# ScalarE keeps the turned tokens of two tiles whole from PSUM, in place of GpSimd's sums of heads and rests

## The chip, the cores and the metric

One core of a Trainium2 chip runs the whole program. The time is device microseconds (us) of one execution; the median of the runs counts.

## What is computed

A decoder trunk of two layers on 512 tokens of width 1024, all in float32. Each layer has a mixer (attention of some kind with an output projection) and a gated MLP with a causal convolution of width 3. Each is followed by a residual and a LayerNorm:

```python
for i in range(DEPTH):
    m = even_mixer(x, ...) if i % 2 == 0 else odd_mixer(x, ...)
    x = layer_norm(DEEPNORM_ALPHA * x + m, ln_mix_g[i], ln_mix_b[i])
    f = conv_ffn(x, w_up[i], conv_w[i], conv_b[i], w_down[i])
    x = layer_norm(DEEPNORM_ALPHA * x + f, ln_ffn_g[i], ln_ffn_b[i])
```

`conv_ffn` multiplies by `w_up` (1024 x 5632), convolves along the tokens, forms silu(gate) * value and multiplies by `w_down`.

## The kernel before

**Heads and rests.** TensorE multiplies in a format with fewer bits than float32. So each operand is kept as a head (`_hi`, the rounded value) and a rest (`_lo`, the value less the head), and each product is three matmuls: head by head, head by rest, rest by head. For the weights, ScalarE makes the heads (`heads`, L490) and GpSimd the rests (`rest`, L336, in two halves of 1024 columns). The weights come from memory in steps, numbered through the program; AT_UP is the first step of the up projection in a layer, AT_UP+1 the second.

**The LayerNorms.** There are four, i = 0 to 3; i = 0 and 2 follow the mixers, and the MLP of the layer comes behind them. The 512 tokens are four tiles t = 0 to 3 of 128. On VectorE `norm(i)` goes, for each tile, through `norm_sum` (L948, residual plus product out of two banks, then the mean L955), `norm_mul` (L968, which reads `x` and `gain`), `norm_root` (L976, L979, L982, each one element wide) and `norm_out` (L991, which reads `ln_mul` and `shift` and gives `xn`). ScalarE makes the statistics in between (`norm_stats`, L514 to L520).

**Turning.** TensorE turns each normalised tile (`turn_x(i, t)`, L1376, eight transposes) into banks 2t and 2t+1. It waits for `xn` of the tile. ScalarE makes the heads `xt_hi` of the turned tokens (`xt_heads`, L507), VectorE the rests `xt_lo` (`xt_rests`, L934). The order of work on every engine is written out by hand: each engine runs its own list, in order, and waits on semaphores. VectorE's order in `norm` is: ... `norm_sum(2)`, `xt_rests(0)`, `xt_rests(1)`, `norm_mul(2)`, `norm_root(2)`, `norm_out(2)`, `norm_sum(3)`, `norm_mul(3)`, `norm_root(3)`, `norm_out(3)`, `xt_rests(2)`, `xt_rests(3)`.

**The up projection.** TensorE begins it while the last tiles are still being normalised: `first_columns` (L1434) multiplies step AT_UP with the first 256 tokens, unit 0, then turns tile 2, then unit 1; then `up_half(0, 0)` multiplies the first half of step AT_UP+1 with the same tokens into bank 2, tile 3 is turned, and `up_half(0, 1)` multiplies the second half into bank 3. Then the same follows for the other 256 tokens. A unit of 24 matmuls on 256 tokens is one such multiplication. All further steps (`up_body`) use a scheme with seven products instead of eight (two by two blocks, the tokens as left and right half, the 1024 inputs as low and high half), L1765. It needs sums and differences of weights and of tokens. The mixed tokens are T1 to T4 in `t_raw`, made on VectorE by `tokens_mixed` (L1239 to L1247) from the turned tokens of tiles 2 and 3 in banks 4 to 7, and from those of tiles 0 and 1. The latter are no longer in their banks by then. They stand in `x_raw`, 128 x 2 x 8 x 128 float32. GpSimd makes `x_raw` (`token_sum`, L432) as the sum of `xt_hi` and `xt_lo`, two operations of 128 x 1024 in each layer. The scheme's weights are the blocks W11, W12, W22 and four sums of blocks; their rests are made by GpSimd (`w_rest`, L445) and VectorE (L1258), their heads by ScalarE (L765; W11's first one at L921).

GpSimd's list around the change: the rests of AT_UP and AT_UP+1 (L336), a wait for `xn` of all four tiles, `token_sum(0)`, `token_sum(1)`, W11's rest (L445), then the rests of T3 and T4 of tile 2 and of tile 3 (L438), each after its head.

ScalarE's list around the change: `norm_stats(0)`, `norm_stats(1)`, `xt_heads(0)`, `xt_heads(1)`, `norm_stats(2)`, `heads(after + 1)` (this is step AT_UP+1), `norm_stats(3)`, `xt_heads(2)`, a load of the table for Silu (L916), W11's head (L921), `xt_heads(3)`, the copies out of banks 4 and 6 into `t_raw` (L839).

Of the kernel before, what the change touches and what calls it, by code (L numbers as in the profile page):

```python
# [22 lines left out]
F32 = mybir.dt.float32  # L23
F32R = mybir.dt.float32r
ACT = mybir.ActivationFunctionType
ALU = mybir.AluOpType

P = 128
# [4 lines left out]
NT = S // P  # L33
# [51 lines left out]
def build(nc, x_in, xt_in, w_stream, ident_in, rope_in, mask_in, tri_in, conv_in, ln_in, out):  # L85
    ctx = ExitStack()
    with ctx:
# [6 lines left out]
        bank = [ctx.enter_context(nc.psum_tensor(f"bank{b}", [P, 512], F32)) for b in range(8)]  # L94
# [7 lines left out]
        xt_hi = sb("xt_hi", [P, KD, S], F32R)  # L102
        xt_lo = sb("xt_lo", [P, KD, S], F32R)
# [7 lines left out]
        x = sb("x", [P, NT, D])  # L111
# [45 lines left out]
        with ExitStack() as st:  # L157
            sb("below_x_raw", [P, KF - 4, S], stack=st)
            x_raw = sb("x_raw", [P, 2, KD, P], stack=st)
# [169 lines left out]
        def _(pool):  # L329
# [29 lines left out]
            for l in range(DEPTH):  # L359
# [67 lines left out]

                w, u = W[l], U[l]

                def token_sum(j):  # L430
                    pool.wait_ge(T[2 * l + 1]["lo"], 2 * j + 2)
                    pool.tensor_tensor(x_raw[:, j, :, :], xt_hi[:, :, j * P:(j + 1) * P].bitcast(F32),  # L432
                                       xt_lo[:, :, j * P:(j + 1) * P].bitcast(F32), ALU.add).then_inc(w["x"], 1)

                def t_rest(row, j, seen):
                    part = slice(j * P, (j + 1) * P)
                    pool.wait_ge(*w.at("th", seen))
# [14 lines left out]
                    pool.tensor_tensor(h_all[:, f, :], sig[f % 2][:, :], cv[f % 2][:, :],  # L452
                                       ALU.mult).then_inc(u["h"], 1)

                pool.wait_ge(N[2 * l]["xn"], NT)
                token_sum(0)
                token_sum(1)
                w_rest(0, W11, w_raw[(b + AT_UP + FIRST) % 2][:, 0:Q])
                for j in range(2):
                    t_rest(T3, j, 4 * j + 1)  # L460
# [24 lines left out]
        def _(act):  # L485
# [18 lines left out]
            def xt_heads(i, t):  # L504
                act.wait_ge(T[i]["mm"], t + 1)
                for g in range(2):
                    act.activation(xt_hi[:, 4 * g:4 * g + 4, t * P:(t + 1) * P],  # L507
                                   bank[2 * t + g][:, :].rearrange("p (k q) -> p k q", k=4),
                                   ACT.Copy).then_inc(T[i]["hi"], 1)

            def norm_stats(i, t):
                n = N[i]
                act.wait_ge(n["mean"], t + 1)
                act.activation(ln_junk[:, :], x[:, t, :], ACT.Square, bias=stat[:, t, 2:3],  # L514
                               accum_out=stat[:, t, 3:4]).then_inc(n["sq"], 1)
                act.wait_ge(n["sq"], t + 1)
                act.activation(stat[:, t, 4:5], stat[:, t, 3:4], ACT.Ln, bias=eps[:, 0:1],
                               scale=4.0 / D).then_inc(n["lv"], 1)
                act.wait_ge(n["lv"], t + 1)
                act.activation(stat[:, t, 5:6], stat[:, t, 4:5], ACT.Exp, scale=-0.5).then_inc(n["y0"], 1)  # L520
# [155 lines left out]
            for l in range(DEPTH):  # L676
# [53 lines left out]
                w, u = W[l], U[l]  # L730
                for i, after in ((2 * l, b + AT_O + 4), (2 * l + 1, b + PER_LAYER)):
# [160 lines left out]
                    if i == 2 * DEPTH - 1:  # L892
                        def scaled(t):
                            act.wait_ge(N[i]["nt"], 2 * t + 2)
                            act.wait_ge(N[i]["mulg"], t + 1)
                            act.activation(x[:, t, :], product(i, t), ACT.Copy,
                                           scale=stat[:, t, 8:9]).then_inc(N_LAST["scaled"], 1)

                        norm_stats(i, 0)
                        norm_stats(i, 1)  # L900
                        scaled(0)
                        scaled(1)
                        norm_stats(i, 2)
                        norm_stats(i, 3)
                    else:
                        norm_stats(i, 0)
                        norm_stats(i, 1)
                        xt_heads(i + 1, 0)
                        xt_heads(i + 1, 1)
                        norm_stats(i, 2)  # L910
                        act.wait_ge(w_used, after - 1)
                        heads(after + 1, used=False)
                        norm_stats(i, 3)
                        xt_heads(i + 1, 2)
                        if i % 2 == 0:
                            act.preload_act_table(ACT.Silu)  # L916
                            first = after + FIRST
                            s, part = operand(l, W11)
                            act.wait_ge(raw_full[first % 2], filled(first, 0))
                            act.wait_ge(w_used, after)  # L920
                            act.activation(w_hi[s][:, part], w_raw[first % 2][:, 0:Q], ACT.Copy).then_inc(w["hi"], 1)  # L921
                        xt_heads(i + 1, 3)
                        if i % 2:
                            act.wait_ge(N[i]["xn"], NT)
                            load_gain(i + 1)
# [3 lines left out]
        def _(dve):  # L929
            def xt_rests(i, t):  # L930
                for g in range(2):
                    dve.wait_ge(T[i]["hi"], 2 * t + g + 1)
                    part = xt_hi[:, 4 * g:4 * g + 4, t * P:(t + 1) * P]
                    dve.tensor_tensor(xt_lo[:, 4 * g:4 * g + 4, t * P:(t + 1) * P],  # L934
                                      bank[2 * t + g][:, :].rearrange("p (k q) -> p k q", k=4),
                                      part.bitcast(F32), ALU.subtract).then_inc(T[i]["lo"], 1)

            def norm_sum(i, t, halves=(0, 1)):

                n = N[i]  # L940
                for g in halves:
                    if (i, t, g) == (0, 0, 0):
                        dve.wait_ge(x_full, 16 * NT)
                    if t < NT - 1 or g == 0 and i == 2 * DEPTH - 1:
                        dve.wait_ge(n["rows"], t + 1)
                    else:
                        dve.wait_ge(w_used, i // 2 * PER_LAYER + (PER_LAYER if i % 2 else AT_UP))
                    dve.scalar_tensor_tensor(out=x[:, t, g * HALF:(g + 1) * HALF],  # L948
                                             in0=x[:, t, g * HALF:(g + 1) * HALF], scalar=ALPHA,
                                             in1=bank[2 * t + g][:, :], op0=ALU.mult, op1=ALU.add,  # L950
                                             accum_out=stat[:, t, g:g + 1]).then_inc(n["sum"], 1)
                if halves[-1] == 0:
                    return
                dve.wait_ge(n["sum"], 2 * t + 2)
                dve.tensor_scalar(stat[:, t, 2:3], stat[:, t, 0:1], stat[:, t, 1:2], -1.0 / D,  # L955
                                  ALU.add, ALU.mult).then_inc(n["mean"], 1)
# [38 lines left out]
            def norm(i):  # L995
                norm_sum(i, 0)
                norm_mul(i, 0)
                norm_sum(i, 1)
                norm_root(i, 0)
                norm_out(i, 0)  # L1000
                norm_mul(i, 1)
                norm_root(i, 1)
                norm_out(i, 1)
                norm_sum(i, 2)
                xt_rests(i + 1, 0)
                xt_rests(i + 1, 1)
                norm_mul(i, 2)
                norm_root(i, 2)
                norm_out(i, 2)
                norm_sum(i, 3)  # L1010
                norm_mul(i, 3)
                norm_root(i, 3)
                norm_out(i, 3)
                xt_rests(i + 1, 2)
                xt_rests(i + 1, 3)
# [356 lines left out]
        def _(pe):  # L1372
# [49 lines left out]
            def col_unit(c, it, u, out_bank, tile_done, half=None, part=slice(None)):  # L1422

                s = slot(c)
                tok = slice(0, S) if half is None else slice(half * S // 2, (half + 1) * S // 2)
                todo = []
                for k in range(KD):
                    at = slice(u * UNIT + k * P, u * UNIT + (k + 1) * P)
                    todo += [(w_hi[s][:, at], xt_hi[:, k, tok]), (w_hi[s][:, at], xt_lo[:, k, tok]),
                             (w_lo[s][:, at], xt_hi[:, k, tok])]  # L1430
                for n, (w, m) in list(enumerate(todo))[part]:
                    if n == 0:
                        pe.wait_ge(lo_ready, 2 * (whole(c) + 2 * it) + u + 1)
                    mm = pe.matmul(out_bank[:, tok], w, m, start=n == 0, stop=n == len(todo) - 1)  # L1434
                    if n == len(todo) - 1 and half != 0:

                        mm.then_inc(w_used if u else tile_done, 1)
                    yield mm
# [222 lines left out]
            for l in range(DEPTH):  # L1661
# [135 lines left out]

                def up_half(half, unit):

                    for _ in col_unit(b + AT_UP + 1, 0, unit, bank[2 + unit], U[l]["g_mm"], half):  # L1800
                        pass

# [107 lines left out]
```

## Time and profile before

| | |
|---|---|
| median of 3 runs | 1187.87 us (1187.16 to 1187.98) |
| the profiled execution's own time | 1187.65 us |
| its span in the profile | 1185.8 us |
| TensorE busy | 1171.5 us, 99% |
| VectorE, ScalarE, GpSimd busy | 718.1, 636.4, 678.0 us |
| chain that ended last | TensorE 88%, VectorE 8%, GpSimd 2% |

Times of rows are microseconds from the span's start. PE is TensorE, PEld its weight loads, DVE VectorE, ACT ScalarE, POOL GpSimd. A row of a timeline gives start, duration, engine, line, operation, output and inputs, how many are merged, and in brackets the idle time before it with its releaser. The duration of an instruction includes the time in which it has been issued and can't proceed.

### The profile page before, as it was taken

The numbers are of one execution on the slowest core, as the hardware profiler recorded it, in microseconds if no ns is written. First come the engines' busy times: TensorE is split into PE (matmuls) and PEld (weight loads), VectorE is DVE, ScalarE is ACT, GpSimd is POOL, SyncE is SP. The second block draws the span as 40 slices with busy tenths as digits, with TensorE's granted clock in tenths as the row PEclk, the third lists the DMA queues.
The fourth block names the chain that finished last, engine by engine and source line by source line (L and its number), as shares of the span: only waits on it lengthen the run. The fifth ranks groups of instructions, "written<-read, shape, count | busy, mean of one in ns | idle before, by whom it ended". The sixth has DMA issues, their size and how long they took to land.

```text
span 1185.8 us, 19571 instructions
## 1 busy us (share of the span) xinstructions
PE 1171.5 (99%) x7384; PEld 1033.5 (87%) x7384; DVE 718.1 (61%) x1378; ACT 636.4 (54%) x1105; POOL 678.0 (57%) x422
## 2 busy tenths in 40 slices
PE   9999999999999999999999999999999999999997
PEld 8777777799999999888888888888999999998885
DVE  4045556299988888322370465554999888872126
ACT  4256676356666666422342577663676666652223
POOL 4545554247877777655514333323787777765462
PEclk9999999999999999999999999999999999999999
DMA  8321222321323222422323121113133222343211
GB/s 304 148 90 67 103 74 102 108 82 51 128 106 106 102 98 96 166 72 105 120 94 109 71 72 58 49 72 107 37 107 109 104 106 107 106 141 107 106 71 72
DMA packets 20616, 119.51 MB, mean 101 GB/s; under 512 B 2512, under 2 KB 2896, under 8 KB 8144
## 3 DMA queue, kind: packets, MB, share of 16 engines
q1 hardware_dynamic: 18832, 113.78, 26.7%
q10 hardware_dynamic: 1728, 5.03, 1.3%
q8 instruction: 30, 0.49, 0.2%
q14 instruction: 26, 0.21, 0.1%
HBM read 112.51 MB, written 2.10 MB: 97 GB/s over the span
## 4 chain that ended last, share of the span: by engine, by line
PE 88%; DVE 8%; POOL 2%; ACT 1%; issue 1%; DMA 0%; DVEq 0%; SPq 0%; ACTq 0%; POOLq 0%
PE bank L1765 32%; PE bank L1403 31%; PE bank L1434 14%; PE bank L1544 2%; PE bank L1530 2%; PE bank L1600 1%; PE bank L1560 1%; PE bank L1623 1%; POOL w_lo L336 1%; PE bank L1462 1%; DVE qs_raw L1298 1%; PE bank L1610 1%; PE bank L1657 1%; PE bank L1376 1%; DVE ln_mul L968 1%
## 5 line engine op out<-in xcount | busy, mean ns | idle before, releaser
L336 POOL TENSOR_TENSOR w_lo<-w_raw,w_hi 128x1024 fp32r<-128x1024 f32 x110 | 281.7, 2580 | 302.9 <-ACT w_hi L490 259.5
L490 ACT ACTIVATE w_hi<-w_raw 128x2048 fp32r<-128x2048 f32 x52 | 99.3, 1911 | 171.4 <-PE bank L1403 157.0
L1765 PE MATMUL bank<-t_hi,w_hi 128*128 128x256 f32 x640 | 181.5, 284 | 0.4 <-DVE w_lo L1258 0.4
L1765 PE MATMUL bank<-t_lo,w_hi 128*128 128x256 f32 x640 | 181.3, 283 | 0.0
L1765 PE MATMUL bank<-t_hi,w_lo 128*128 128x256 f32 x640 | 181.3, 283 | 0.0
L445 POOL TENSOR_TENSOR w_lo<-w_raw,w_hi 128x512 fp32r<-128x512 f32 x120 | 156.1, 1301 | 19.7 <-ACT w_hi L765 18.7
L1403 PE MATMUL bank<-w_hi,a_hi 128*128 128x512 f32 x480 | 153.2, 394 | 0.3 <-POOL w_lo L336 0.2
L1403 PE MATMUL bank<-w_hi,a_lo 128*128 128x512 f32 x480 | 153.1, 392 | 0.0
L1403 PE MATMUL bank<-w_lo,a_hi 128*128 128x512 f32 x480 | 152.3, 391 | 0.0
L445 POOL TENSOR_TENSOR w_lo<-qs_raw,w_hi 128x512 fp32r<-128x512 f32 x80 | 104.1, 1301 | 71.1 <-ACT w_hi L765 71.1
L1337 DVE TENSOR_TENSOR a_lo<-h_all,a_hi 128x1024 fp32r<-128x1024 f32 x22 | 48.0, 2180 | 153.5 <-ACT a_hi L739 153.5
L1765 PE MATMUL bank<-xt_hi,w_hi 128*128 128x256 f32 x480 | 136.2, 284 | 2.0 <-POOL w_lo L445 2.0
L1434 PE MATMUL bank<-xt_hi,w_hi 128*128 128x512 f32 (+1 forms) x384 | 138.1, 360 | 0.0
L1765 PE MATMUL bank<-xt_hi,w_lo 128*128 128x256 f32 x480 | 136.0, 283 | 0.0
L1765 PE MATMUL bank<-xt_lo,w_hi 128*128 128x256 f32 x480 | 135.9, 283 | 0.0
L1434 PE MATMUL bank<-xt_lo,w_hi 128*128 128x512 f32 (+1 forms) x384 | 135.7, 353 | 0.0
L1434 PE MATMUL bank<-xt_hi,w_lo 128*128 128x512 f32 (+1 forms) x384 | 134.9, 351 | 0.0
L1765 PEld LDWEIGHTS bank<-t_hi,w_hi 128*128 128x128 f32 x640 | 122.9, 192 | 0.8 <-DVE w_lo L1258 0.8
L1765 PEld LDWEIGHTS bank<-t_lo,w_hi 128*128 128x128 f32 x640 | 123.0, 192 | 0.0
L1765 PEld LDWEIGHTS bank<-t_hi,w_lo 128*128 128x128 f32 x640 | 122.9, 192 | 0.0
L1403 PEld LDWEIGHTS bank<-w_hi,a_lo 128*128 128x128 f32 x480 | 90.2, 188 | 19.8 <-issue 0.7
L1403 PEld LDWEIGHTS bank<-w_lo,a_hi 128*128 128x128 f32 x480 | 90.1, 188 | 19.5 <-issue 0.6
(156 smaller groups left out, 2523.9 us busy)
## 6 DMA issues: line engine op xcount, KB each, us to landing
w_raw<-w_stream SPq DMA_DIRECT2D x97, 1024.0 KB, 4.8
qs<-qc SPq DMA_DIRECT2D x16, 128.0 KB, 2.0
ks<-kc SPq DMA_DIRECT2D x16, 128.0 KB, 2.0
x<-x_in SPq DMA_DIRECT2D x4, 512.0 KB, 5.0
gain<-ln_in ACTq DMA_DIRECT2D x4, 512.0 KB, 4.9
shift<-ln_in ACTq DMA_DIRECT2D x4, 512.0 KB, 6.1
x<-xt_in SPq DMA_DIRECT2D x3, 512.0 KB, 8.5
out<-x SPq DMA_DIRECT2D x3, 512.0 KB, 2.6
```

The costliest lines, as they stand in the source:

```text
L336: pool.tensor_tensor(w_lo[slot(c)][:, part], w_raw[s][:, part], w_hi[slot(c)][:, part].bitcast(F32), ALU.subtract).then_inc(lo_ready, 1)
L445: pool.tensor_tensor(w_lo[s][:, part], src, w_hi[s][:, part].bitcast(F32), ALU.subtract).then_inc(w["lo_p"], 1)
L490: act.activation(w_hi[slot(c)][:, :], w_raw[c % 2][:, :], ACT.Copy).then_inc(hi_ready, 2)
L968: dve.scalar_tensor_tensor(out=product(i, t), in0=x[:, t, :], scalar=stat[:, t, 2:3], in1=gain[:, :], op0=ALU.add, op1=ALU.mult).then_inc( ...
L1298: dve.tensor_tensor(qs_raw[c % 2][:, n, :], raw[:, 2 * n * Q:(2 * n + 1) * Q], raw[:, 3 * Q:4 * Q], ALU.add).then_inc(w["qs"], 1)
L1337: dve.tensor_tensor(a_lo[:, k:k + 2, :], h_all[:, bass.ds(2 * j, 2), :], a_hi[:, k:k + 2, :].bitcast(F32), ALU.subtract).then_inc(DN[l]["a ...
L1376: mm = pe.transpose(bank[2 * t + k // 4][:, (k % 4) * P:(k % 4 + 1) * P], x[:, t, k * P:(k + 1) * P], ident[:, :])
L1403: mm = pe.matmul(bank[2 * t + g][:, :], lhs, w[s][:, u * UNIT + g * HALF:u * UNIT + (g + 1) * HALF], start=first and n == 0, stop=end and ...
L1434: mm = pe.matmul(out_bank[:, tok], w, m, start=n == 0, stop=n == len(todo) - 1)
L1530: mm = pe.matmul(bank[2 + h][:, at:at + L], q[p][part, qi * P:(qi + 1) * P], k[p][part, 0:L], start=n == 0, stop=n == 2)
L1544: mm = pe.transpose(bank[4 + h][:, m * P:(m + 1) * P], probs[h][qi % 2][:, k * P:(k + 1) * P], ident[:, :])
L1765: mm = pe.matmul(out, lhs[s][:, at], rhs[:, k, :], start=(k, v) == (0, 0), stop=(k, v) == (3, 2))
```

## The change

GpSimd's `token_sum` and its wait for all of `xn` are taken out. ScalarE gets `keep_whole(l, t)`, two copies of 128 x 512 out of banks 2t and 2t+1 into `x_raw`, behind `xt_heads` of the same tile; for tile 1 it stands behind `norm_stats(2)` and ahead of `heads(after + 1)`, with a wait for the rests of tiles 0 and 1. VectorE waits for tile 0's copy before `xt_rests(0)`, since TensorE's next product into banks 0 and 1 waits for these rests. TensorE waits for both copies in `up_half`, which writes banks 2 and 3. This is done for i = 0 and 2 alone. The count of `x` and its waits in `tokens_mixed` are as before.

```diff
-                def token_sum(j):
-                    pool.wait_ge(T[2 * l + 1]["lo"], 2 * j + 2)
-                    pool.tensor_tensor(x_raw[:, j, :, :], xt_hi[:, :, j * P:(j + 1) * P].bitcast(F32),
-                                       xt_lo[:, :, j * P:(j + 1) * P].bitcast(F32), ALU.add).then_inc(w["x"], 1)
-
...
-                pool.wait_ge(N[2 * l]["xn"], NT)
-                token_sum(0)
-                token_sum(1)
                 w_rest(0, W11, w_raw[(b + AT_UP + FIRST) % 2][:, 0:Q])
...
+            def keep_whole(l, t):
+                for g in range(2):
+                    kept = act.activation(x_raw[:, t, 4 * g:4 * g + 4, :],
+                                          bank[2 * t + g][:, :].rearrange("p (k q) -> p k q", k=4), ACT.Copy)
+                kept.then_inc(W[l]["x"], 1)
...
                         xt_heads(i + 1, 0)
+                        if i % 2 == 0:
+                            keep_whole(l, 0)
                         xt_heads(i + 1, 1)
                         norm_stats(i, 2)
+                        if i % 2 == 0:
+                            act.wait_ge(T[i + 1]["lo"], 4)
+                            keep_whole(l, 1)
                         act.wait_ge(w_used, after - 1)
                         heads(after + 1, used=False)
...
                 norm_sum(i, 2)
+                if i % 2 == 0:
+                    dve.wait_ge(*W[i // 2].at("x", 1))
                 xt_rests(i + 1, 0)
...
                 def up_half(half, unit):
 
+                    pe.wait_ge(*w.at("x", 2))
                     for _ in col_unit(b + AT_UP + 1, 0, unit, bank[2 + unit], U[l]["g_mm"], half):
```

## Rows read from the trace of the kernel before

**Rows 1.** The page: its first part, and its fourth by engine.

```profile
PE 1171.5 (99%) x7384; PEld 1033.5 (87%) x7384; DVE 718.1 (61%) x1378; ACT 636.4 (54%) x1105; POOL 678.0 (57%) x422
...
PE 88%; DVE 8%; POOL 2%; ACT 1%; issue 1%; DMA 0%; DVEq 0%; SPq 0%; ACTq 0%; POOLq 0%
```

**Rows 2.** The chain of waits, both layers: start, us, what.

```profile
255.70 5.71 PE bank L1434 x48
...
261.42 1.10 PE bank L1376 x8
...
838.24 1.10 PE bank L1376 x8
```

**Rows 3.** Waits of PE and PEld, whole span: us in total, times, longest.

```profile
PE bank L1765 <- POOL w_lo L445: 2.0, 2, 1.0
...
PEld bank L1376 <- DVE x L991: 0.8, 3, 0.3
```

**Rows 4.** Timeline of ScalarE, layer 0.

```profile
249.29 1.09 ACT L507 ACTIVATE xt_hi<-bank 128x512 fp32r<-128x512 f32 x2 [2.55 <-PE bank L1376]
...
251.97 1.90 ACT L490 ACTIVATE w_hi<-w_raw 128x2048 fp32r<-128x2048 f32 x1
255.73 1.15 ACT L514 ACTIVATE ln_junk<-x,stat 128x1024 f32<-128x1024 f32 x1 [1.86 <-DVE stat L955]
...
259.82 0.63 ACT L921 ACTIVATE w_hi<-w_raw 128x512 fp32r<-128x512 f32 x1
262.55 1.09 ACT L507 ACTIVATE xt_hi<-bank 128x512 fp32r<-128x512 f32 x2 [2.09 <-PE bank L1376]
263.52 1.09 ACT L839 ACTIVATE t_raw<-bank 128x512 f32<-128x512 f32 x2
```

**Rows 5.** Timeline of GpSimd, layer 0; the second row is the first's second half.

```profile
253.95 5.88 POOL L336 TENSOR_TENSOR w_lo<-w_raw,w_hi 128x1024 fp32r<-128x1024 f32 x2 [15.44 <-ACT w_hi L490]
...
256.45 3.38 POOL L336 TENSOR_TENSOR w_lo<-w_raw,w_hi 128x1024 fp32r<-128x1024 f32 x1
...
261.44 4.76 POOL L432 TENSOR_TENSOR x_raw<-xt_hi,xt_lo 128x1024 f32<-128x1024 f32 x2 [1.61 <-DVE x L991]
...
268.86 1.29 POOL L438 TENSOR_TENSOR t_lo<-t_raw,t_hi 128x512 fp32r<-128x512 f32 x1
```

**Rows 6.** Timeline of VectorE, layer 0: the norms of tiles 2 and 3.

```profile
252.95 1.28 DVE L991 SCALAR_TENSOR_TENSOR x<-ln_mul,stat,shift 128x1024 f32<-128x1024 f32 x1
254.15 0.68 DVE L948 SCALAR_TENSOR_TENSOR x<-x,bank 128x512 f32<-128x512 f32 x1
...
255.74 1.83 DVE L968 SCALAR_TENSOR_TENSOR ln_mul<-x,stat,gain 128x1024 f32<-128x1024 f32 x1
...
257.67 2.18 DVE L979 SCALAR_TENSOR_TENSOR stat<-stat 128x1 f32<-128x1 f32 x1
259.88 0.16 DVE L982 SCALAR_TENSOR_TENSOR stat<-stat 128x1 f32<-128x1 f32 x1
260.08 1.28 DVE L991 SCALAR_TENSOR_TENSOR x<-ln_mul,stat,shift 128x1024 f32<-128x1024 f32 x1
```

**Rows 7.** Tiles w_lo and stat, whole span: ns min/median/max, first and last start.

```profile
L336 POOL TENSOR_TENSOR w_lo<-w_raw,w_hi x110: 2354/2396/3407, 16.5 to 1154.7; 128x1024 fp32r<-128x1024 f32 x110
...
L968 DVE SCALAR_TENSOR_TENSOR ln_mul<-x,stat,gain x16: 1276/1285/2462, 238.2 to 1180.1; 128x1024 f32<-128x1024 f32 x16
...
L979 DVE SCALAR_TENSOR_TENSOR stat<-stat x16: 219/220/2181, 241.1 to 1181.5; 128x1 f32<-128x1 f32 x16
```

**Rows 8.** Timelines of GpSimd and VectorE, layer 0, first sums of weights.

```profile
270.12 1.74 POOL L438 TENSOR_TENSOR t_lo<-t_raw,t_hi 128x512 fp32r<-128x512 f32 x1
...
269.68 1.02 DVE L1298 TENSOR_TENSOR qs_raw<-w_raw 128x512 f32<-128x512 f32 x1
270.63 1.78 DVE L1298 TENSOR_TENSOR qs_raw<-w_raw 128x512 f32<-128x512 f32 x1
```

**Rows 9.** A stretch near the end: us, busy us (x instructions), PEclk, DMA.

```profile
1180.00:1182.00 2.00, 0.00 (x0) 0.00 (x0) 1.90 (x6) 0.74 (x4) 0.00 (x0) 1.00 0.52 211
```

## The prediction

> **What bounds the kernel now.** Four views, in this order. The page's first and fourth part: TensorE is busy 99% of the span and is 88% of the chain that ended last, VectorE 8% [rows 1]. So a cost counts only where it makes TensorE wait, and a saving only where TensorE waits today. Second, the chain of waits around the edit, after the mixer of each layer: TensorE runs 48 matmuls of `up_half`/`first_columns` without a gap from 255.70 for 5.71 us, and at 261.42 turns token tile 3 (`turn_x(i, 3)`); in layer 1 the same step stands at 838.24, 576.82 us later [rows 2]. Third, the waits: the weight load of that turning is released by VectorE's `norm_out` (L991), 0.8 us in three such waits, 0.3 the longest; the only other waits of TensorE near the edit are 2.0 us in two (1.0 each) on GpSimd's L445 [rows 3]. So at 261.42 VectorE is exactly on time: its L991 runs from 260.08 for 1.28 us, to 261.36 [rows 6], and there is no slack. Fourth, the timelines of ScalarE, GpSimd and VectorE over the same 15 us [rows 4 to 6]. They show what makes VectorE so late: its two-input operations take turns with GpSimd's. L968 takes 1.83 us instead of its usual 1.285, and L979, one element wide, takes 2.18 instead of 0.22 [rows 6, 7]; L979 ends at 259.85, and GpSimd's second half of L336 ends at 259.83 (256.45 + 3.38) [rows 5, 6]. L948, which reads one operand from SBUF and one from a bank, takes 0.68 beside the same GpSimd operation [rows 6].
>
> **What is removed.** The two `token_sum` of each layer, 4.76 us of GpSimd from 261.44 [rows 5], and with them GpSimd's wait for tile 3's `xn`. After them stand W11's rest, T3's first rest and T4's first rest, each 1.29 us; the last begins at 268.86 [rows 5], later than 266.20 + 2 x 1.29 = 268.78 at which GpSimd would reach it, so it waits for ScalarE's head and not for GpSimd. So the 4.76 us become idle time in front of T4, and the later GpSimd rests, with TensorE's waits of 1.0 us behind them, come no sooner, since all they need comes from VectorE. VectorE never waited for `x_raw` either: 261.44 + 4.76 = 266.20 is before its first use of tile 1's. **Gain: 0.**
>
> **ScalarE's first copy** (`keep_whole(l, 0)`). Nearest row: the pair of copies from banks to `t_raw`, two instructions, 1.09 us [rows 4]; the pair of `xt_heads` before it has the same length, and what follows it starts 0.97 after it (262.55 to 263.52). The copy stands where ScalarE is idle for 2.55 us up to 249.29, so behind heads that end at 246.74 [rows 4]: from 246.62 (the same overlap of 0.12) to 247.71. VectorE's `xt_rests(0)` now waits for it, by less than 0.97 us, since it waited for the heads just ahead before. Then VectorE waits for ScalarE's heads of tile 1 (from 249.29) anyway. Cost 0; without that cover up to 0.97 us in each layer.
>
> **ScalarE's second copy.** It stands right before `heads(after + 1)`, the heads of step AT_UP+1, which starts at 251.97 with no idle time ahead of it and takes 1.90 [rows 4]. Its own wait for `lo` is met by then (VectorE does the rests of tile 1 before `norm_mul(2)`, 1.285 us, and that before L991 at 252.95, so they are done before 251.7 [rows 6, 7]). So these heads end 0.97 later, at 254.84 instead of 253.87. ScalarE itself recovers in its 1.86 us idle before 255.73 [rows 4], so the statistics of tile 3, the table load and W11's head (259.82 + 0.63 = 260.45) keep their times [rows 4]. TensorE's new wait for `x` is met at 253.06; `up_half` is the second half of the 48 matmuls and begins at 255.70 + 5.71 / 2 = 258.55, 5.5 us later. The load of the stream behind these rests is issued 0.8 us later by SP's queue; it is step AT_UP+3, and all of AT_UP+2 comes before its use. All of that costs 0.
>
> **What the 0.97 us do to GpSimd and VectorE.** Today the first rest of AT_UP+1 starts at 253.95 beside VectorE's L991 (252.95 + 1.28 = 254.23), and GpSimd's second half follows after 2.50 us where an undisturbed one takes 2.40 and is followed after 2.36 [rows 5 to 7]. Now it starts at 254.92 with nothing in its way and ends at 257.32 instead of 256.49: **0.83 us later**. L968, issued at 255.74, ended 1.08 after it (257.57) and will end at 258.40. GpSimd's second half, queued behind L968, ended 2.26 after that and will end at 260.66. L979, queued behind it, ends at 260.68 instead of 259.85. TensorE needs the first half at 258.5 and the second after the turning, so it waits for neither; it waits for L991.
>
> **W11's rest in the gap.** This is the larger term. Until now GpSimd stood still from 259.83 until `xn` of tile 3, 1.61 us [rows 5], so L982 (0.16) and L991 (1.28) ran alone [rows 6]. With the wait gone, W11's rest comes directly behind: its head is there at 260.45, so it starts at 260.62 and, at 1.29 us (the T4 rest of the same width in [rows 5]), ends at 261.91. L982 can be issued only when L979 has ended, at about 260.71, and then stands behind it. The row that prices this is a few us later: GpSimd's rest issued at 270.12 is held up by VectorE's first sum and then runs before VectorE's second sum, issued at 270.63, which takes 1.78 us instead of 0.68; each side gets one turn [rows 8]. So L982 ends at about 261.93 instead of 260.04, 1.89 later. If instead L982 slips in first, L991 stands behind the rest: it ends 1.08 after 261.91, at 262.99 instead of 261.36, 1.63 later. I take 1.85, near the first, because in [rows 8] the engine whose operation was queued first had the turn, and GpSimd's is queued 0.09 us ahead.
>
> The Trainium skill, in "SBUF — State Buffer", on port contention, says that a VectorE instruction with two SBUF inputs and a GpSimd instruction that reads SBUF exclude each other for the whole instruction, and that issue order decides who waits. The trace agrees: 2.18 us for an operation of 0.22. The page speaks against this change: it would add the same 1.3 us turn of W11, and by it alone the sum would be the same.
>
> **The sum.** VectorE's chain from L991 on is unbroken until TensorE's first wait on L445 in `up_body` (turning, `xt_rests`, the mixed tokens, the first sums), so the whole of it, and TensorE with it, moves by the same 1.85; nothing later gives it back, and the 1.0 us wait on L445 stays. Two layers: 2 x 1.85 = 3.7 us. The profiled execution took 1187.65 us (span 1185.8 and 1.85 around it), 0.22 below the median of 1187.87. From its own time: 1187.65 + 3.7 = 1191.35; against the median 1191.6. I forecast **1191.5 us**.
>
> **The rivals.**
> A, only the shift: W11's rest doesn't get between (VectorE's three short steps keep the turn). The cost is 0.83 in each layer, 1.66 in all: 1189.5 us, within the bound and so not slower. It decides at one point, 260.6 to 260.9: if L982 and L991 are both taken up before GpSimd reads. For it: nothing in this trace shows GpSimd queued behind a VectorE operation as short as L979. Against it: [rows 8], and that GpSimd queued at 253.95 lost only about 0.1 us, so it asks at its start.
> B, everything is hidden: TensorE's turning has cover that I don't see. Then 1187.9. Against: the wait for L991 in [rows 3].
> C, it is faster: GpSimd's freed 4.76 us bring T3 and T4 of the turned tokens and W12's rest sooner and take away the two waits of 1.0 us: 1185.9 at best, if the shift is hidden too. Against: T4 waits for its head [rows 5].
> D, TensorE's clock: each gap at `turn_x` grows to about 2 us. In this trace the granted clock is still 1.00 (2.4 GHz) at the end of a stretch of 2 us without any matmul [rows 9], so I expect it to hold. If it fell to 1.2 GHz for the length of one 24-matmul unit (half of 5.71), that unit would take up to 2.9 us more, 5.7 in two layers: 1197 us. The Trainium skill, "TensorE: Matmul & The Clock Gate", says that idle time halves the clock; the row above speaks against so short a gap doing it.
> E, the change doesn't do what it says: `x_raw` is then copied elsewhere or not in time. The new waits stand in front of every reader, so at most a wait shows; it has no chance of its own.
>
> **How the numbers follow.** Forecast 0.70, A 0.14, B 0.08, C 0.03, D 0.05. A measurement of this kernel can tell about 0.2% from no change, 2.4 us. Slower by more: forecast and D, 0.75. Within: A and B, 0.22. Faster: 0.03. The range takes in the forecast between its ends (2 x 1.63 and 2 x 1.89, with 0.4 us for the spread of runs) and A: 1189.1 to 1192.6; it leaves out B, C and D, 0.16.
>
> **What the changed profile would show.** ScalarE: two pairs of copies into `x_raw` of 1.09 us at about 246.6 and 252.0, the heads of AT_UP+1 at 252.9. GpSimd: its rests at 254.9 and 257.3, W11's rest at 260.6 and not at 266.2, then idle until the head of T3. VectorE: L979's line ends near 260.7, and L982's takes over 1 us instead of 0.16 (or L991's over 2 instead of 1.28). TensorE: the turning of tile 3 at about 263.3 after a wait of 2 us for VectorE, and the same in layer 1. A turning at 262.3 would mean A, one at 261.4 B; wrong altogether would be a wait of TensorE on `x`, or heads of AT_UP+1 that don't move.

## The result, and the profile after

The changed kernel took 1193.03 us (median of 6, 1191.55 to 1193.59) against 1187.72 for the kernel before measured beside it (median of 6): ratio 1.0043, 95% interval 1.0033 to 1.0054. So it is 5.3 us slower. The forecast was 1191.5 with an upper end of 1192.6. Two more sets of five runs of the same kernel, taken later, gave 1193.1 against 1187.61 (ratio 1.0039, 1.0026 to 1.0053) and, on another chip, 1191.85 against 1187.75 (1.0036, 1.0023 to 1.0050). Line numbers after the change: L499 is `xt_heads`, L505 `keep_whole`, L482 the heads of weights, L971 `norm_mul`, L982 and L985 the last two steps of `norm_root`, L994 `norm_out`, L1381 the turning, L440 GpSimd's rests of the scheme's weights, L1770 the scheme's products. In the runs further down the same lines stand a few numbers off.

The page of the changed kernel, its first part and its fourth by engine, against [rows 1]:

```profile
PE 1173.5 (99%) x7384; PEld 1035.3 (87%) x7384; DVE 722.2 (61%) x1378; ACT 640.3 (54%) x1113; POOL 668.6 (56%) x418
...
PE 87%; DVE 9%; POOL 2%; ACT 1%; issue 1%; DMA 0%; DVEq 0%; SPq 0%; ACTq 0%; POOLq 0%
```

GpSimd lost 9.4 us of work, ScalarE took on 3.9, VectorE shows 4.1 more though it got none: that is time in which it stood issued and blocked (the rows below show 2 x 1.87 of it).

The timelines of the changed kernel in layer 0, ScalarE, GpSimd, VectorE and TensorE; they answer [rows 4 to 6] and [rows 2]. The whole stretch begins 0.56 us later than before (the turning of tile 0 at 245.14 against 244.58), in a part of the program that the change does not touch: of the thirteen kernels traced here this turning stood between 244.12 and 245.59.

```profile
252.53 1.07 ACT L505 ACTIVATE x_raw<-bank 128x512 f32<-128x512 f32 x2
253.48 1.92 ACT L482 ACTIVATE w_hi<-w_raw 128x2048 fp32r<-128x2048 f32 x1
...
255.47 5.75 POOL L336 TENSOR_TENSOR w_lo<-w_raw,w_hi 128x1024 fp32r<-128x1024 f32 x2 [16.41 <-ACT w_hi L482]
261.17 1.28 POOL L440 TENSOR_TENSOR w_lo<-w_raw,w_hi 128x512 fp32r<-128x512 f32 x1
...
256.29 2.66 DVE L971 SCALAR_TENSOR_TENSOR ln_mul<-x,stat,gain 128x1024 f32<-128x1024 f32 x1
...
259.05 2.19 DVE L982 SCALAR_TENSOR_TENSOR stat<-stat 128x1 f32<-128x1 f32 x1
261.27 1.20 DVE L985 SCALAR_TENSOR_TENSOR stat<-stat 128x1 f32<-128x1 f32 x1
262.51 1.28 DVE L994 SCALAR_TENSOR_TENSOR x<-ln_mul,stat,shift 128x1024 f32<-128x1024 f32 x1
...
263.85 1.09 PE L1381 MATMUL bank<-ident,x 128*128 128x128 f32 x8 [1.88 <-DVE x L994]
```

To be seen: the heads start behind the copy; `norm_mul` takes 2.66 us where [rows 6] had 1.83; W11's rest now stands at 261.17, directly behind the rests of AT_UP+1; and the step L985, one element wide, takes 1.20 instead of 0.16. `norm_out` starts at 262.51 instead of 260.08. Less the 0.56 this is **1.87 us**, and TensorE waits 1.88 for it.

Layer 1 of the changed kernel, timelines of VectorE and TensorE, and two stretches: us, busy us (x instructions) of PE, PEld, DVE, ACT, POOL, then PEclk, DMA share and GB/s.

```profile
839.97 1.20 DVE L985 SCALAR_TENSOR_TENSOR stat<-stat 128x1 f32<-128x1 f32 x1
841.20 1.28 DVE L994 SCALAR_TENSOR_TENSOR x<-ln_mul,stat,shift 128x1024 f32<-128x1024 f32 x1
...
842.54 1.97 PE L1381 MATMUL bank<-ident,x 128*128 128x128 f32 x8 [1.97 <-DVE x L994]
...
842.00:843.00 1.00, 0.46 (x2) 0.46 (x3) 1.00 (x2) 0.00 (x0) 0.00 (x0) 0.74 1.00 426
843.00:844.00 1.00, 1.00 (x7) 1.00 (x6) 0.68 (x2) 0.00 (x0) 0.00 (x0) 0.50 1.04 442
```

`norm_out` starts 4.30 us later than before (841.20 against 836.90): 0.56 + 1.87 + 1.87. But now something new: the granted clock falls to 0.50 (1.2 GHz) at 842.4, at the end of the gap, and the turning takes 1.97 us instead of 1.09, 0.88 more, with ScalarE's heads and VectorE's rests waiting behind it.

The waits of TensorE in the changed kernel, against [rows 3]:

```profile
PE bank L1381 <- DVE x L994: 3.9, 2, 2.0
...
PE bank L1770 <- POOL w_lo L440: 1.3, 2, 1.0
```

The profiled execution took 1193.02 us, 5.37 more than that of before. The parts: 0.56 before the first turning, 1.87 and 1.87 at the two turnings, 0.88 by the clock in layer 1. The wait for GpSimd in layer 1 is 0.35 us instead of 1.0: TensorE gets there later through the slow matmuls and finds more of the work done. The remaining 0.2 stands in the last norm, where VectorE takes 7.15 us instead of 6.91 from the first sum of tile 2 to its `norm_out`. The runs with the wait put back, with the late copy and with 12 fill matmuls show the same 7.15, the one with W11's rest early (made from the kernel before) 6.95. In the changed kernel `norm_mul` of tile 2 takes 2.33 us instead of 2.09 behind GpSimd's L473, which starts later because `norm_root` of tile 0 was late: its L982 starts 0.47 us after ScalarE's last statistics step has ended, where it was 0.12 before. Why it does stays open.

### The profile page after: what moved, and what is told of

The parts are those of the page before. It is cut to its first block, busy times and chain, and to the rows that moved or that the text cites. A ratio compares the mean times of both kernels' runs of the same rounds, so it can differ in the third digit from the quotient of the medians.

```text
span 1191.2 us, 19583 instructions
## 1 busy us (share of the span) xinstructions
PE 1173.5 (99%) x7384; PEld 1035.3 (87%) x7384; DVE 722.2 (61%) x1378; ACT 640.3 (54%) x1113; POOL 668.6 (56%) x418
## 4 chain that ended last, share of the span: by engine, by line
PE 87%; DVE 9%; POOL 2%; ACT 1%; issue 1%; DMA 0%; DVEq 0%; SPq 0%; ACTq 0%; POOLq 0%
PE bank L1770 32%; PE bank L1408 31%; PE bank L1439 13%; PE bank L1549 2%; PE bank L1535 2%; PE bank L1605 1%; PE bank L1565 1%; PE bank L1628 1%; POOL w_lo L336 1%; DVE ln_mul L971 1%; PE bank L1467 1%; DVE x L994 1%; DVE qs_raw L1303 1%; DVE stat L982 1%; PE bank L1615 1%
## 5 line engine op out<-in xcount | busy, mean ns | idle before, releaser
L482 ACT ACTIVATE w_hi<-w_raw 128x2048 fp32r<-128x2048 f32 x52 | 99.3, 1912 | 171.4 <-PE bank L1408 157.7
L1770 PE MATMUL bank<-t_hi,w_hi 128*128 128x256 f32 x640 | 181.3, 283 | 0.4 <-DVE w_lo L1263 0.4
L1770 PE MATMUL bank<-t_lo,w_hi 128*128 128x256 f32 x640 | 181.1, 283 | 0.0
L1770 PE MATMUL bank<-t_hi,w_lo 128*128 128x256 f32 x640 | 181.1, 283 | 0.0
L440 POOL TENSOR_TENSOR w_lo<-w_raw,w_hi 128x512 fp32r<-128x512 f32 x120 | 156.1, 1302 | 19.7 <-ACT w_hi L763 18.7
L440 POOL TENSOR_TENSOR w_lo<-qs_raw,w_hi 128x512 fp32r<-128x512 f32 x80 | 104.2, 1302 | 71.1 <-ACT w_hi L763 71.1
L1770 PE MATMUL bank<-xt_hi,w_hi 128*128 128x256 f32 x480 | 136.0, 283 | 1.3 <-POOL w_lo L440 1.3
L1770 PE MATMUL bank<-xt_hi,w_lo 128*128 128x256 f32 x480 | 135.8, 283 | 0.0
L1770 PE MATMUL bank<-xt_lo,w_hi 128*128 128x256 f32 x480 | 135.8, 283 | 0.0
L1770 PEld LDWEIGHTS bank<-t_hi,w_hi 128*128 128x128 f32 x640 | 122.9, 192 | 0.8 <-DVE w_lo L1263 0.8
L1770 PEld LDWEIGHTS bank<-t_lo,w_hi 128*128 128x128 f32 x640 | 122.9, 192 | 0.0
L1770 PEld LDWEIGHTS bank<-t_hi,w_lo 128*128 128x128 f32 x640 | 122.9, 192 | 0.0
```

The costliest lines, as they stand in the source:

```text
L440: pool.tensor_tensor(w_lo[s][:, part], src, w_hi[s][:, part].bitcast(F32), ALU.subtract).then_inc(w["lo_p"], 1)
L482: act.activation(w_hi[slot(c)][:, :], w_raw[c % 2][:, :], ACT.Copy).then_inc(hi_ready, 2)
L1770: mm = pe.matmul(out, lhs[s][:, at], rhs[:, k, :], start=(k, v) == (0, 0), stop=(k, v) == (3, 2))
```

## The experiments

**What makes 1.87 us.** The theory: two turns of the port that VectorE's two-input operations and GpSimd's reads take one after the other; the late heads cost 0.83, W11's rest in the gap about 1.02 (1.85 less 0.83). The rivals: the late heads alone, or W11's rest alone.

The first puts the wait back:

```diff
+                pool.wait_ge(N[2 * l]["xn"], NT)
                 w_rest(0, W11, w_raw[(b + AT_UP + FIRST) % 2][:, 0:Q])
```

> The changed kernel with GpSimd's wait for xn of all four tiles put back ahead of W11's rest. Theory (two turns taken from VectorE): the heads of AT_UP+1 are still 0.97 us late, so L979's counterpart ends 0.83 us late, but W11's rest stands outside the gap and the short step after it takes 0.16 us again. TensorE's wait at the turning of tile 3 is about 1.0 us in each layer, and the clock stays at 1.00 there. Time: 1187.7 + 2 x 0.83 = 1189.4. Rival (the late heads alone carry the cost, W11's rest is harmless): the time stays near 1193. Second rival (something at the start of the program, 0.56 us in the profile, belongs to the change): 1190.0.

Measured: 1189.47 against 1188.12, ratio 1.0014 (1.0005 to 1.0023): 1.35 us. VectorE, GpSimd and TensorE in layer 0:

```profile
260.29 0.16 DVE L986 SCALAR_TENSOR_TENSOR stat<-stat 128x1 f32<-128x1 f32 x1
260.49 1.29 DVE L995 SCALAR_TENSOR_TENSOR x<-ln_mul,stat,shift 128x1024 f32<-128x1024 f32 x1
...
261.85 1.28 POOL L440 TENSOR_TENSOR w_lo<-w_raw,w_hi 128x512 fp32r<-128x512 f32 x1 [1.61 <-DVE x L995]
...
261.83 1.09 PE L1382 MATMUL bank<-ident,x 128*128 128x128 f32 x8 [0.85 <-DVE x L995]
```

The short step is back at 0.16 us. This execution's first turning of the stretch stood at 244.15, 0.43 earlier than before's, so `norm_out` at 260.49 is 0.84 late, as the sum had it. Most of the loss goes with one wait put back, so the late heads alone don't carry the cost. Nor do the 0.56 us at the start belong to the change, as the second rival has it: here the stretch began earlier than before. (The measured interval by itself would not tell 1189.4 from 1190.0.)

The second leaves the wait out and moves the copy instead:

```diff
-                        if i % 2 == 0:
-                            act.wait_ge(T[i + 1]["lo"], 4)
-                            keep_whole(l, 1)
                         act.wait_ge(w_used, after - 1)
                         heads(after + 1, used=False)
+                        if i % 2 == 0:
+                            act.wait_ge(T[i + 1]["lo"], 4)
+                            keep_whole(l, 1)
```

> The changed kernel with the copy of tile 1 moved behind the heads of AT_UP+1; W11's rest still has no wait ahead. Theory: the heads are on time again, GpSimd's second half ends at about 259.8 on the old time scale, and W11's head comes at 260.45, when VectorE's short steps are over and norm_out is under way; so W11's rest waits for norm_out and not the other way round. Both costs vanish: 1187.7, TensorE's waits at the turning 0.2 us. Rival (W11's rest takes its turn by itself): about 2 x 1.1 us more, 1189.9.

Measured: 1188.12 against 1188.12, ratio 1.0001 (0.9992 to 1.0010). VectorE and GpSimd, layer 0:

```profile
260.10 1.29 DVE L994 SCALAR_TENSOR_TENSOR x<-ln_mul,stat,shift 128x1024 f32<-128x1024 f32 x1
...
260.55 1.97 POOL L440 TENSOR_TENSOR w_lo<-w_raw,w_hi 128x512 fp32r<-128x512 f32 x1 [0.69 <-ACT w_hi L924]
```

Here the same unguarded rest does no harm: its head comes at about 260.5, `norm_out` has been running since 260.10, and now it is GpSimd that is blocked (1.97 us instead of 1.29). So the two parts are not independent. The late heads cost 0.84, and they also push the short steps to where W11's rest is ready, which costs the other 1.03.

The third does the second part alone, in the kernel before, with W11's rest and its head made early:

```diff
+                w_rest(0, W11, w_raw[(b + AT_UP + FIRST) % 2][:, 0:Q])
                 pool.wait_ge(N[2 * l]["xn"], NT)
                 token_sum(0)
                 token_sum(1)
-                w_rest(0, W11, w_raw[(b + AT_UP + FIRST) % 2][:, 0:Q])
...
-                        xt_heads(i + 1, 2)
                         if i % 2 == 0:
-                            act.preload_act_table(ACT.Silu)
                             first = after + FIRST
...
                             act.activation(w_hi[s][:, part], w_raw[first % 2][:, 0:Q], ACT.Copy).then_inc(w["hi"], 1)
+                        xt_heads(i + 1, 2)
+                        if i % 2 == 0:
+                            act.preload_act_table(ACT.Silu)
```

> The kernel before, with W11's rest moved ahead of GpSimd's wait and of the sums, and its head moved on ScalarE ahead of the heads of turned tile 2, so that it is ready when GpSimd's second half ends. The heads of AT_UP+1 are where they were. Theory: the one step L982 takes about 1.2 us in place of 0.16 and TensorE waits about 1.2 us at each turning of tile 3; 1187.7 + 2 x 1.1 = 1189.9. Rival (VectorE keeps its turn between short steps, and the late end of the changed kernel has another cause): 1187.7.

Measured: 1190.24 against 1188.12, ratio 1.0019 (1.0010 to 1.0029): 2.1 us. GpSimd and VectorE, layer 0:

```profile
259.33 1.29 POOL L445 TENSOR_TENSOR w_lo<-w_raw,w_hi 128x512 fp32r<-128x512 f32 x1
...
259.42 1.22 DVE L983 SCALAR_TENSOR_TENSOR stat<-stat 128x1 f32<-128x1 f32 x1
260.67 1.28 DVE L992 SCALAR_TENSOR_TENSOR x<-ln_mul,stat,shift 128x1024 f32<-128x1024 f32 x1
```

A step one element wide takes 1.22 us instead of 0.16, with the heads of AT_UP+1 where they were, and TensorE waits 1.07 and 1.15 us at the two turnings. This is the price of one turn, 1.06 us, by itself, and rival A of the prediction (the short steps keep the port) is gone.

**What makes the rest.** The theory: TensorE's clock, which falls in the gap. It was tried by filling the gap:

```diff
+                        if i % 2:
+                            pe.wait_ge(N[i - 1]["mean"], NT)
+                            for _ in range(12):
+                                pe.matmul(bank[7][:, 0:P], ident[:, :], ident[:, :], start=True, stop=True)
                         turn_x(i, 3)
```

> The changed kernel with 12 matmuls of 128 columns (identity by identity, into bank 7 before the turning overwrites it) on TensorE right before the turning of tile 3 in both layers; they fill some 1.3 of the 1.9 us in which it waits there. Theory (the part above 2 x 1.87 us is TensorE's clock, which falls to 1.2 GHz in the gap in layer 1 of the profiled execution and costs about 0.9 us of VectorE's chain there): the granted clock stays 1.00 through both turnings, and the time is 1187.7 + 3.7 = 1191.5. Rival (the clock costs nothing that the chain behind doesn't hide, and the rest is in the start of the program or elsewhere): it stays at 1193.0.

Measured: 1193.09 against 1188.12, ratio 1.0043 (1.0030 to 1.0057): no gain. TensorE in layer 1:

```profile
840.95 2.84 PE L1461 MATMUL bank<-ident 128*128 128x128 f32 x24
843.63 1.04 PE L1381 MATMUL bank<-ident,x 128*128 128x128 f32 x8
```

The clock stayed at 1.00 and the turning took 1.04, but the fill was mis-sized: each of the 12 shows as two instructions (x24), so it lasted 2.68 us and ended 0.6 after `norm_out` (841.74 + 1.29 = 843.03). What was won was spent. So again with 7, beside the changed kernel:

> The changed kernel once more, as the measure for the next run on the same chip. Theory: about 5.3 us above the kernel before (ratio 1.0044), of which 2 x 1.87 us stand in VectorE's chain ahead of the two turnings and the rest comes from TensorE's clock after a gap of 2 us in at least one layer. If the fall depends on where the gap lies in time, single times scatter over more than 1 us, with the lowest near 3.7 us above before.

> The changed kernel with 7 matmuls of 128 columns before the turning of tile 3 in both layers. In the run with 12 each took 0.223 us (two passes), 2.7 us together, so they ended 0.6 us behind norm_out in each layer and hid the effect of the clock; 7 take 1.56 us and end before it. Theory (the clock's fall is the part above 2 x 1.87): the granted clock is 1.00 throughout, and the time is 1.2 to 1.6 us below that of the changed kernel on the same chip, 3.7 above the kernel before. Rival (the clock's fall is hidden or the rest is elsewhere): equal to the changed kernel within 0.3 us.

Measured: the changed kernel 1193.1, ratio 1.0039, single times 1191.53, 1191.64, 1193.10, 1193.44, 1193.45; with the fill 1192.22 (1191.69 to 1192.53), ratio 1.0035 (1.0022 to 1.0049). That is 0.9 us below the changed kernel, where 1.2 to 1.6 were expected, and 4.6 above the kernel before instead of 3.7. The run with 7 also changed a part of layer 1's projection by 5 matmuls, so it was made anew:

> The changed kernel with 7 matmuls of 128 columns before the turning of tile 3 in both layers and nothing else changed. (The run before with 7 had also 7 in place of 12 matmuls of the value projection beside the turning of layer 1's last tile, so its difference wasn't that of the fill alone.) Theory (TensorE's clock falls in the gap in most executions, and this is the part above 2 x 1.87): the clock is 1.00 throughout, single times scatter like those of the kernel before, about 1.5 us, with none of the upper values of the changed kernel, and the median is 3.7 us above before. Rival (the clock's fall costs nothing): equal to the changed kernel in the next run.

> The changed kernel beside the run with 7 matmuls, on the same chip. Theory: single times in two groups, about 4 and 5.5 us above the kernel before; the profiled execution has its granted clock at 0.5 after a turning exactly if it belongs to the upper group.

Measured on one chip, before at 1187.75: with the fill 1192.7 (1191.78 to 1192.74), ratio 1.0041 (1.0027 to 1.0055); the changed kernel 1191.85 (1191.69 to 1192.37). By these medians the fill gains nothing, against the expectation: it is 4.95 us above the kernel before, not 3.7, and 0.85 above the changed kernel. The expectation of the third set failed too: its five times form one group, 3.9 to 4.6 above the kernel before, and its profiled execution, the third fastest of them, has the clock at 0.50. Its trace tells why that cost little: the clock fell in layer 0, at 264.8, after the turning. TensorE's turning, then a stretch behind it:

```profile
263.49 1.09 PE L1381 MATMUL bank<-ident,x 128*128 128x128 f32 x8 [1.89 <-DVE x L994]
...
265.00:267.00 2.00, 2.00 (x11) 2.00 (x11) 1.75 (x3) 1.69 (x4) 0.00 (x0) 0.50 0.01 4
```

The turning took its usual 1.09 us; the slow matmuls behind it ran while VectorE's chain went on, and one of TensorE's two later waits of 1.0 us for GpSimd is gone in this execution. `norm_out` of layer 1 is 4.03 late here, 0.20 of it at the start and 3.75 by the two turnings, so the fall cost 0.1. It costs only where it covers the turning: 0.88 in the first profile, where it came 0.1 us before the turning; 0.65 in the second (1.74 instead of 1.09), where it came at 843.1, 0.2 us into the turning; almost none in the third. Of the 16 executions of the changed kernel 8 lie above 1192.74; none of the 10 with seven fill matmuls does. That fits, but 5 of these had the other edit as well, and the start of the program moves every execution: the turning of tile 0 stood between 244.12 and 245.59 in the thirteen traces, as wide as the single times of the kernel before (1187.16 to 1188.65). For the profiled executions that start can be taken out: time less the turning of tile 0, against the same difference of the kernel before (1187.65 - 244.58).

| kernel | profiled execution, us | turning of tile 0 | above before, start taken out |
|---|---|---|---|
| changed, three sets | 1193.02, 1193.10, 1191.85 | 245.14, 245.50, 244.78 | 4.81, 4.53, 4.00 |
| seven fill matmuls alone | 1191.78 | 244.75 | 3.96 |
| late copy | 1187.97 | 244.59 | 0.31 |

With 3.74 for the two turnings and 0.2 for the last norm, 0.9, 0.6 and 0.1 are left for the clock in the three, and 0.0 with the fill; the rows of the falls gave 0.88, 0.65 and 0.1. So the clock's part in the profiled executions is shown; its part in the median, between 0 and 0.9 us, stays open, since the set with the fill, whose one trace has no fall of the clock, has a median 4.95 above before all the same.

**What the change could be worth.** GpSimd is to be quiet while VectorE does its short steps, and the turning is to come as soon as the tile is there. From the kernel with the late copy:

```diff
-                rest(b + AT_UP + 1)
+                rest(b + AT_UP + 1, 0, (0,))
+                pool.wait_ge(N[2 * l]["xn"], NT)
+                rest(b + AT_UP + 1, 0, (1,))
```

> The changed kernel with the copy of tile 1 behind the heads of AT_UP+1, and GpSimd's wait for xn of all tiles put ahead of the second half of the rests of AT_UP+1, so that GpSimd stands still during VectorE's norm_root and norm_out of tile 3. TensorE's list is unchanged. Theory: L979's counterpart takes 0.22 us instead of 2.18 and norm_out ends about 2 us earlier, but TensorE has 24 matmuls to finish before the turning, so only the 0.2 us at the turning are gained in each layer: 1187.7 to 1187.9 where before is 1188.1. Rival (the freed time reaches the two waits of 1.0 us on GpSimd's L445): 1186.

Measured: 1187.78 against 1187.61, ratio 0.9998 (0.9989 to 1.0007). VectorE and TensorE, layer 0, in an execution whose stretch began 1.01 late:

```profile
259.13 1.28 DVE L996 SCALAR_TENSOR_TENSOR x<-ln_mul,stat,shift 128x1024 f32<-128x1024 f32 x1
...
262.26 1.04 PE L1383 MATMUL bank<-ident,x 128*128 128x128 f32 x8
```

`norm_out` is 1.96 us earlier (260.08 + 1.01 - 259.13), and next to nothing comes of it, since TensorE turns the tile at the same place of its list, 1.85 us after it is ready. So the place was moved too (the marked lines are against the run just shown):

```diff
-                    for _ in col_unit(b + AT_UP + 1, 0, unit, bank[2 + unit], U[l]["g_mm"], half):
-                        pass
+                    for n, _ in enumerate(col_unit(b + AT_UP + 1, 0, unit, bank[2 + unit], U[l]["g_mm"], half)):
+                        if (half, unit, n) == (0, 0, 8):
+                            turn_x(2 * l + 1, 3)
...
-                        turn_x(i, 3)
+                        if i % 2 == 0:
+                            turn_x(i, 3)
```

> As the run before, with TensorE's turning of tile 3 moved into up_half(0, 0), behind its 8th of 24 matmuls, in both layers; after the second norm it stays where it was. Theory: VectorE's chain from the turning on starts about 2 us earlier, which is more than TensorE's later waits of 1.0 and 0.2 us in each layer: these go, and with 0.2 us at the turning about 1.2 to 1.4 us are gained in each layer: 1185.5 to 1185.8 where before is 1188.1. Rival (the chain is then held by the units of matmuls that ScalarE's first gate and value columns wait for, so that the later waits stay): 1187.7.

Measured: **1184.46** against 1187.61, ratio 0.9972 (0.9960 to 0.9983), 3.1 us faster than the kernel before and more than expected. The waits of TensorE for other engines over the whole span, all of its entries but two of 1.1 and 0.7:

```profile
PE bank L1410 <- POOL w_lo L336: 1.3, 3, 0.6
```

The entries for the scheme's products (2.0 and 0.5 us in the kernel with the late copy) and for the turning are gone. The move of the turning by itself was not run; in the kernel before, `norm_out` ends at 261.36, just before the old place, so a turning moved forward alone would wait for it. Does this need ScalarE's copies? The same two edits in the kernel before, with GpSimd's sums:

> The kernel before, with GpSimd's sums kept, and the two edits of the fastest run so far: GpSimd's wait for xn ahead of the second half of the rests of AT_UP+1, and the turning of tile 3 behind the 8th matmul of up_half(0, 0). ScalarE copies nothing whole. It tells whether ScalarE's copies are worth anything once VectorE's chain is shorter. Theory: yes, a little: the sums end at about 266.6 on GpSimd, W11's rest and T3's follow until 269, T4's and the second tile's end about 2 us later against VectorE's chain than in the fastest run, and VectorE's reads of x_raw wait for the sums (tile 0's by about 1.5 us, tile 1's likewise); about 1 to 2 us in each layer are lost again: 1186 to 1188. Rival (GpSimd has room for the sums anyway): as fast as the fastest run, 3.1 us below before.

Measured: 1186.65 against 1187.75, ratio 0.9991 (0.9982 to 1.0000). VectorE in layer 0, and a wait of TensorE:

```profile
264.76 0.69 DVE L1243 TENSOR_TENSOR t_raw<-bank,x_raw 128x512 f32<-128x512 f32 x1 [1.20 <-POOL x_raw L434]
...
PE bank L1767 <- POOL w_lo L447: 1.3, 2, 0.7
```

VectorE now waits 1.20 us for GpSimd's sum and TensorE again for rests, and about 2 us of the 3.1 are lost; what is left, 1.1 us, has an interval that reaches to no change. So the sums had room only in a chain that was late for another reason.

## Why the prediction was right and wrong

The gain of 0 for the removed sums held: T4's first rest still starts with its head (271.30), and TensorE's wait of 1.0 us on GpSimd stayed in layer 0 (in layer 1 the slow matmuls took 0.65 us of it). The first copy cost nothing: VectorE waited 0.18 us for it and then 0.88 for the next heads. The shift was forecast at 0.83 and measured at 0.84 in the run with the wait put back; W11's turn at 1.02 (1.06 at its upper end) and measured at 1.03, by itself at 1.06. The sum at each turning was forecast at 1.85 and is 1.87, in both layers. The Trainium skill's rule on the shared port ("SBUF — State Buffer", section "Who interferes with whom"), that a VectorE instruction with two SBUF inputs and a GpSimd instruction that reads SBUF exclude each other and the order of issue decides who is blocked, is borne out by both orders: GpSimd's rest blocked VectorE's step in the changed kernel, VectorE's `norm_out` blocked the same rest with the late copy.

The step that failed is the sum: it is 2 x 1.85 for the blocked VectorE chain and nothing else. It puts at nothing what the longer gap does to TensorE's clock, and it counts the spread of executions as 0.4 us. Three terms are missing.

First, rival D. From [rows 9] the prediction argued that 2 us without a matmul leave the clock at 1.00, and gave the fall 0.05. In all three profiled executions of the changed kernel the clock fell in or right behind one of the two gaps of 1.9 to 2.0 us. The row was misread as well. These lines of the same trace stand around it, the last matmul and the next two stretches:

```profile
1177.08 0.40 PE L1403 MATMUL bank<-w_hi,a_lo 128*128 128x512 f32 x1
...
1182.00:1183.00 1.00, 0.00 (x0) 0.00 (x0) 1.00 (x2) 0.00 (x0) 0.00 (x0) 0.90 0.28 111
1183.00:1186.00 3.00, 0.00 (x0) 0.00 (x0) 0.31 (x1) 0.00 (x0) 0.00 (x0) 0.50 0.47 175
```

So TensorE had been idle for 4.5 us at the end of the row, not 2, and the clock was at 0.50 in the stretch from 1183: the trace before showed the clock falling in idle time. The price was wrong too: what counts is not the slower unit of matmuls (2.9 us) but the turning alone (0.65 to 0.88), since VectorE's chain goes through it, while the unit behind it has slack, TensorE's later wait of 1.0 us.

Second, the spread was taken from three runs; the start of the stretch alone differs by 1.5 us between traces, and it stood 0.56 later in the profiled execution of the changed kernel. Third, 0.2 us in the last norm were not foreseen. The upper end of the range also doesn't follow from its working: 1187.87 + 2 x 1.89 + 0.4 is 1192.05, not 1192.6.

So the mechanism of the 3.7 us and its size were right, in both layers. The profiled execution, at 1193.02, would have been inside the range without the clock's 0.88 (1192.14) or without the 0.56 of the start (1192.46); it took both to leave it. The medians of the three sets lie 0.4 to 1.8 us above the 3.74 of the turnings; how that divides between clock and start, the runs don't show.

## What to carry to other kernels

Before work is handed to an engine that looks idle, look at what stands behind the insertion point: one microsecond in front of the heads of one step of weights moved GpSimd's next operations onto VectorE's critical steps. A wait that seems to be of no use may be what keeps two engines off a shared port; here the wait for `xn` was worth 1.03 us in each layer. Ask what a gap brings with it: beside the 3.7 us of waiting, the lower clock behind it took up to 0.9 more in one execution. Where a chain has been shortened, move the consumer's place in its list too, since the shorter chain alone brought nothing that could be measured and both together 3.1 us.

## What the runs showed of the hardware

An operation of VectorE one element wide with two SBUF inputs waits for a whole turn of GpSimd: 1.20 to 1.22 us instead of 0.16 beside a rest of 128 x 512, 2.18 instead of 0.22 beside one of 128 x 1024. In three of the six gaps of 1.9 to 2.0 us in an otherwise full TensorE stream (two gaps in each of three executions) the granted clock went to 0.50 at the gap's end or up to 1.3 us behind it. In the four gaps of 0.85 to 1.15 us (the runs with the wait put back and with W11's rest early) and in the four that seven matmuls had cut to 0.3 to 0.4 us it stayed at 1.00.
